# First attention: split values as the stationary operand, scaled probabilities of two token tiles as the moving one

## The reference, cut to what matters

```python
p = jax.nn.softmax(logits, axis=-1)
return jnp.einsum('bqhk,bqkhd->bqhd', p.astype(v.dtype), v_sel)
...
mixed = jnp.concatenate([a_out.reshape(b, s, D_A) * jax.nn.silu(za),
                         b_out.reshape(b, s, D_B) * jax.nn.silu(zb)], axis=-1)
x = x + jnp.einsum('bse,ed->bsd', mixed, w_out[layer])
```

## Time and profile before

| | |
|---|---|
| times of three runs | 1032.04, 1032.56, 1034.12 us; median 1032.56 us |
| the profiled execution | 1032.51 us, of which the span (first to last instruction) 1030.7 us |
| TensorE busy | 1019.2 us, 99% of the span |
| VectorE, ScalarE, GpSimd busy | 665.9 us (65%), 534.4 us (52%), 365.7 us (35%) |
| first attention (first score at 169.9 us, last value product ends just before 299.8 us) | TensorE busy 131.5 of the 132.5 us from 169.7 to 302.2 |
| second attention | 512 to 607 us, TensorE busy 93.5 of 95 us |

### The profile page before, as it was taken

The page is one execution under the profiler, slowest core; times in us unless marked ns, Lnnn a source line. Parts: engine busy times, 40 slices in busy tenths (PEclk is TensorE's granted clock), DMA queues, the critical chain, the costliest instruction groups (busy, mean ns, idle before and its releaser), DMA issues. The chain is left out here.

```text
span 1030.7 us, 14348 instructions
## 1 busy us (share of the span) xinstructions
PE 1019.2 (99%) x5310; PEld 843.8 (82%) x5310; DVE 665.9 (65%) x1141; ACT 534.4 (52%) x960; POOL 365.7 (35%) x334
## 2 busy tenths in 40 slices
PE   9999999999999999999999999999999999999997
PEld 7788888888878898988887788889888888888885
DVE  5578998675765346824567779444323325999996
ACT  7454445554673255545567884134434436554554
POOL 0022011003330001910165430007779965874562
PEclk9999999999999999999999999999999999999999
DMA  9655332314420285233200362239999951443552
GB/s 335 119 113 119 88 96 67 82 47 130 144 93 1 78 257 164 62 82 82 54 9 1 109 239 62 82 102 322 347 351 333 352 193 62 152 138 138 204 184 82
DMA packets 99637, 146.24 MB, mean 142 GB/s; under 512 B 6208, under 2 KB 60224, under 8 KB 99568
## 3 DMA queue, kind: packets, MB, share of 16 engines
q1 hardware_dynamic: 86016, 129.70, 38.6%
q10 hardware_dynamic: 12768, 12.88, 3.9%
q0 software_dynamic: 784, 2.75, 1.8%
HBM read 123.69 MB, written 21.63 MB: 141 GB/s over the span
## 5 line engine op out<-in xcount | busy, mean ns | idle before, releaser
L2462 DVE TENSOR_TENSOR w_lo<-wring,w_hi 128x1024 fp32r<-128x1024 f32 x32 | 53.0, 1658 | 105.8 <-ACT w_hi L1846 105.8
L1992 DVE TENSOR_TENSOR u_lo<-wring,u_hi 128x1024 fp32r<-128x1024 f32 (+1 forms) x64 | 80.8, 1272 | 50.9 <-ACT u_hi L1540 50.4
L869 PE MATMUL bank<-u_hi,h_hi 128*128 128x512 f32 (+1 forms) x288 | 111.0, 385 | 0.1
L869 PE MATMUL bank<-u_hi,h_lo 128*128 128x512 f32 (+1 forms) x288 | 109.4, 380 | 0.0
L869 PE MATMUL bank<-u_lo,h_hi 128*128 128x512 f32 (+1 forms) x288 | 109.1, 379 | 0.0
L1540 ACT ACTIVATE u_hi<-wring 128x1024 fp32r<-128x1024 f32 (+1 forms) x64 | 65.8, 1033 | 79.1 <-PE bank L869 57.2
L869 PE MATMUL bank<-h_hi,w_hi 128*128 128x512 f32 (+2 forms) x272 | 103.3, 380 | 0.0
L869 PE MATMUL bank<-h_hi,w_lo 128*128 128x512 f32 (+2 forms) x272 | 103.3, 380 | 0.0
L869 PE MATMUL bank<-h_lo,w_hi 128*128 128x512 f32 (+2 forms) x272 | 103.2, 380 | 0.0
L869 PE MATMUL bank<-h_hi,u_hi 128*128 128x512 f32 x224 | 94.4, 421 | 0.4 <-ACT arena L1482 0.2
L1370 PE MATMUL bank<-s_hi,f_hi 128*128 128x512 f32 x224 | 87.5, 391 | 0.7 <-DVE f_lo L2496 0.7
(11 more groups left out here) (374 smaller groups left out, 2543.7 us busy)
## 6 DMA issues: line engine op xcount, KB each, us to landing
wring<-in_w_in SPq DMA_DIRECT2D x60, 512.0 KB, 3.9
wring<-in_w_ff ACTq DMA_DIRECT2D x12, 1024.0 KB, 8.2
wring<-sums_kept SPq DMA_DIRECT2D x16, 768.0 KB, 4.2
wring<-in_w_ff SPq DMA_DIRECT2D x22, 512.0 KB, 6.2
wring<-in_w_ff SPq DMA_DIRECT2D x32, 256.0 KB, 3.3
sums_kept<-wring SPq DMA_DIRECT2D x22, 256.0 KB, 4.9
arena<-in_w_out SPq DMA_DIRECT2D x4, 1024.0 KB, 5.1
wring<-in_w_out SPq DMA_DIRECT2D x2, 2048.0 KB, 13.5
```

Of the source, the lines that this page charges most:

```text
L869: last = mm(b, lhs, rhs, start=(start and n == 0), stop=(stop and n == 2))
L1992: v.tensor_tensor(u_lo[u % RAW_UNITS][:, 0:cols], raw_unit(u), u_hi[u % HI_UNITS][:, 0:cols].bitcast(F32), ALU.subtract).then_inc(u_lo_don ...
L2462: v.tensor_tensor(cut(w_lo[ring3(m)]), src, cut(w_hi[ring3(m)]).bitcast(F32), ALU.subtract).then_inc(w_lo_done, 1)
```

## The change

What it does, part by part:

1. **Value products.** The values are kept split, high and low side by side (`v1_both`), and 128 columns of one head (64 high, 64 low) are the stationary operand. The transposed probabilities are split too (`pt1`), and are the moving operand: 256 columns for the key blocks that both token tiles of a pair (0, 1 or 2, 3) see, 128 for the last. `value1(o, n, r)` makes the whole output of one head for two token tiles. There are 192 matmuls in fp32r instead of 160 in f32.
2. **The output comes turned**, features on partitions. `mixed_transposes` goes. The products with the low halves come out in the upper 64 partitions: ScalarE copies those (`low_rows_of`), VectorE adds them to the lower ones (`collect1`, two additions a call).
3. **Scaling moves ahead of the transposes.** Since the division can't be made on turned outputs, VectorE takes the reciprocals of two steps (32 times) and GpSimd multiplies the 64 probability tiles by them (`scaled`). The transposes wait for `scaled`, and come two steps later than before, in loop t for steps t-4, t-3. The logits have eight buffers instead of four.
4. **Every transposed tile is written twice**, high by ScalarE (`turned_high`, 64 times) and low by VectorE (`turned_low`, 64 times), where one copy was made before.
5. **Room.** The split probabilities take places of the weight ring, so that the gate projections have two raw and two high places (`raw_place`, `hi_place`); their next unit is loaded when the last one but one is used up. Bias strips are loaded per round into two places. The values of vb and va are written by two activations a tile, their low halves by GpSimd (`value_low`). Part of the output weights moves (`late_raw`) and is loaded later, as are x and the first units of the second block.
6. **The end of the loop.** `WO_HIGH` and `ROW_AT` change, ScalarE makes the high half of piece 7 after its loop, the last `mix` is split in two halves, and `first_row` has another order.

```diff
-    WO_HIGH = {46: 0, 48: 1, 50: 2, 53: 3, 55: 4, 59: 5, 61: 6, 63: 7}
+    WO_HIGH = {48: 0, 49: 1, 50: 2, 53: 3, 55: 4, 60: 5, 61: 6}
-    ROW_AT = {58: ((0, 0),), 60: ((0, 1),), 62: ((0, 2),), 64: ((0, 4), (0, 5)), 66: ((0, 3), (1, 0))}
+    ROW_AT = {58: ((0, 0),), 60: ((0, 1),), 62: ((0, 2),), 64: ((0, 3), (0, 4)), 66: ((0, 5), (1, 0)), 68: ((1, 1), (1, 2))}
...
             def turn1(u):
-                pe.wait_ge(e_done, u + 1)
+                i = steps1[u][0]
+                pe.wait_ge(scaled, u + 1)
...
-                for j in range(i + 1):
-                    last = mm(bank[6 + o % 2][:, at:at + HD], probsT1[u % 2][:, j * P:(j + 1) * P],
-                              v1["v" + br][:, j, h * HD:(h + 1) * HD], start=(j == 0), stop=(j == i))
+                both = [(j, part) for j in range(end) for part in ("hi", "lo")]
+                order = both[:-1] + [(end, "hi"), (end, "lo")] + both[-1:]
+                for j, part in order:
+                    first, cols = (0, P) if j == end else (P * (2 * (end - j) - 1), 2 * P)
+                    at = 2 * P * (r + 1) - cols
+                    last = mm(bank[6 + q % 2][:, at:at + cols], v1_both[g][j // 2][:, j % 2, h, :, :].rearrange("p m d -> p (m d)"),
+                              pt1[n, part, r][:, first:first + cols], start=((j, part) == order[0]), stop=((j, part) == order[-1]))
                 last.then_inc(pv_done, 1)
-
-            def mixed_transposes(o):
...
+            for t in range(0, NS + 4, 2):
+                if t >= 4:
+                    turned_high(t - 4)
+                    turned_high(t - 3)
+                if t < NS:
+                    exps(t, steps1, 0, den, logits1)
+                    exps(t + 1, steps1, 0, den, logits1)
+                if t >= 10 and t % NH == 2:
+                    low_rows_of(2 * ((t - 10) // NH))
+                if t >= 16 and t % NH == 0:
+                    low_rows_of(2 * ((t - 16) // NH) + 1)
...
             for t in range(0, NS + 4, 2):
...
+                if t < NS:
+                    score1(t)
+                if 2 <= t < NS + 2:
+                    dve.wait_ge(e_done, t)
+                    v.reciprocal(den[:, t - 2:t], den[:, t - 2:t]).then_inc(rden_done, 1)
+                if t < NS:
+                    score1(t + 1)
+                if t >= 4:
+                    turned_low(t - 4)
+                    turned_low(t - 3)
+                if t >= 12 and t % NH == 4:
+                    collect1(2 * ((t - 12) // NH))
                 if t >= 18 and t % NH == 2:
+                    collect1(2 * ((t - 18) // NH) + 1)
                     mix((t - 18) // NH)
...
+            for u in range(NS):
+                if u % 2 == 0:
+                    pool.wait_ge(rden_done, u // 2 + 1)
+                g.tensor_scalar(logits1[u % 8], logits1[u % 8], den[:, u:u + 1], None, ALU.mult).then_inc(scaled, 1)
+                if u in (9, 11, 13, 15):
+                    value_low("va", (u - 9) // 2)
+                if u + 4 in combos:
+                    combine(u + 4)
```

More of the change, by code:

```diff
@@ L831, in unit_arrived @@
         def unit_arrived(eng, u):
-            eng.wait_ge(unit_in[u % RAW_UNITS], 16 * sum(len(units[m][3]) for m in range(u % RAW_UNITS, u + 1, RAW_UNITS)))
+            eng.wait_ge(unit_in[raw_place(u)], 16 * sum(len(units[m][3]) for m in range(u + 1) if raw_place(m) == raw_place(u)))
         def pair_arrived(eng, m):
@@ L2118, in finish1 @@
[L2118 to L2127 removed]
+                g = t // NH
@@ new lines, in collect1, with mix @@
+            def collect1(q):
+                o, n = q // 2, q % 2
+                dve.wait_ge(lo_rows_done, q + 1)
+                for r in range(2):
+                    cut = slice(2 * P * r, 2 * P * (r + 1))
+                    last = v.tensor_tensor(qk1[r * HD:(r + 1) * HD, o // 4, o % 4, OUTS, 2 * P * n:2 * P * (n + 1)],
+                                           bank[6 + q % 2][0:HD, cut], low_rows1[:, cut], ALU.add)
+                last.then_inc(o_free, 1)
+            def mix(o, cols=slice(0, S)):
@@ L2178, in _ @@
-                for f, tile, k in fill1:
-                    if f in (t, t + 1) and k == KC - 1:
+                for tile in FILL1:
+                    if GATE_AT[tile] in (t, t + 1):
                         gate_rows(tile)
@@ L2193, in _ @@
             mixed_low(6)
-            mix(7)
+            collect1(GROUPS - 2)
+            mix(7, slice(0, S // 2))
             dve.wait_ge(wo_lo_done, 9)
+            mixed_low(7, slice(0, S // 2))
             wo_low(9)
-            mixed_low(7)
-            for m in range(10, 14):
+            for m in (10, 11):
                 wo_low(m)
+            collect1(GROUPS - 1)
+            mix(7, slice(S // 2, S))
+            for m in (12, 13):
+                wo_low(m)
+            mixed_low(7, slice(S // 2, S))
             for u in range(2):
```

398 lines of the change are left out of this document (230 added, 168 removed).

## The result

The changed kernel takes 1068.85 us in the median of four runs (1068.37 to 1070.5), the kernel before in the same session 1032.98 us (1032.04 to 1034.12): a ratio of 1.035 (95%: 1.0332 to 1.0367). The direction is the one I gave the most chance, the size is not: 1038.0 was forecast, and even the upper end of the range, 1047, is 22 us too low.

A forecast was written before the change was run, and what follows sets the result against it. TensorE, busy 1019.2 of 1030.7 us, was taken as the bound. From 1032.5 us: less 17.8 of work and 2.0 of old waits, plus 8 of middle and 17.4 of end waits, gives 1038.1 us; range 1023 to 1047.

The forecast's parts named there:

- TensorE's work, -17.8 us: First attention: 160 f32 products and the mixed transposes removed, 192 products added; 17.8 us less work (16.0 to 17.9).
- the estimate beside it: Price of the 64 short value products by the Trainium skill's 81 ns per matmul: 5.2 us instead of 7.2.
- the page's two signs: Expected on the profile page: TensorE's busy time near 1000 us and its share of the span below 98%.
- Middle rounds of branch b: First attention before loop 56: waits of 0.7 us a round for scores queued behind VectorE's work.
- Middle rounds of branch a: First attention before loop 56: waits of 1.2 us a round, and 2 us in loop 52 behind two output-weight low halves.
- my high end of 13: Waits in the middle rounds, forecast at 8 us: 13 us if the weight ring's transfers come late.
- the two-place weight ring: Middle rounds: ScalarE waits for the next unit's transfer ahead of silu pairs, mostly covered by VectorE's waits; 1 us.
- no bound by itself: GpSimd in the first attention: 16 scalings of each size, 0.77 us for the largest, some 40 us in all.
- The end: Waits from loop 56 on, where no fill work is left: 17.4 us, of which 10.6 us need no backlog.
- P: Start of loop 56, 279.95 us in the trace before; TensorE was forecast to reach loop 64 at P + 14.1.
- Outside the stage: Edits outside the first attention cost nothing; 1 to 3 us if the cover for block two's first units is gone.
- Rival 4: Slower with lower clock: TensorE at 1.2 GHz after two waits of about 5 us, losing 2.5 us each; 1043 us, chance 0.15.

The follow-up runs named there:

- e10: e7 with the four silu pairs of this stage written as copies, leaving the activation out: 1040.26 us against 1042.76.
- e2: Changed kernel with the strips of group 6 and the next weight unit issued ahead of the first two output-weight loads on SP's queue: 1061.67 us.
- e1: Changed kernel with GpSimd's scaling of the probabilities given a second scalar, 1.0: 1062.04 us, 6.8 us less.
- e3: Changed kernel with both the two-scalar scaling and the weight unit issued ahead of the output weights: 1055.68 us.
- e5: e3 with the row terms of loops 64, 66 and 68 behind the transposes and value products instead of ahead: 1047.83 us.
- e9: Kernel before the change, with TensorE made to wait at loop 64 for a chain of three tiny transfers: 1040.03 us against 1032.91.
- e7: e5 with high halves of output weights at loops 47, 49, 51, 53, 55 and pieces 7 and 8 at loop 62: 1042.76 us, 1.0097 of the kernel before.
- e11: e7 with VectorE's `mix` moved from loops 2 modulo 8 to loops 4 modulo 8, behind the scores, except the last but one: 1044.25 us.
- e4: Changed kernel with 106 useless transposes filling TensorE's three long waits at the end of the first attention: 1063.25 us, 5.6 us less.
- e6b: e3 with high halves of output-weight pieces 0 to 4 at loops 50 to 58 and pieces 7 and 8 at loop 62: 1051.18 us.

## Why the prediction was right and wrong, step by step

- **TensorE's work, -17.8 us: borne out where it can be read.** Value products start 0.117 us apart, the short ones of 128 columns too, so the 64 of them are 7.5 us, for the 7.2 forecast and the 5.2 of the estimate beside it; a round of branch b without a long wait takes 15.0 us (212.94 to 227.93), and of that 0.77 us is a wait, which leaves 14.2 us, for the 14.1 forecast. Of the page's two signs, a share below 98% came true (96%) and TensorE near 1000 us busy failed: 1023.5, since work at the low clock is busy for about twice as long.

```profile
212.94 0.75 PEld L1081 LDWEIGHTS bank<-qk_half 64*128 64x128 f32 x12
...
224.04 0.54 PEld L1081 LDWEIGHTS bank<-qk_half 64*128 64x128 f32 x6 [0.77 <-DVE stats L2266]
...
227.93 0.19 PEld L1081 LDWEIGHTS bank<-qk_half 64*128 64x128 f32 x2
```

- **Middle rounds of branch b: right in size, in part by luck.** They take 15.3, 15.6 and 15.0 us, with 0.8 to 1.3 us of waiting in each, against "0.7 us a round" and rounds of "14.8 to 15.5 us". Only the waits at loops 22 and 30 (0.45 and 0.77 us) stand behind `collect1` and `mix`, as forecast; the one at loop 12 (1.18 us) stands behind the low half of a weight unit, and the one at loop 20 (0.84 us) behind a silu pair (see e10).
- **Middle rounds of branch a: mis-sized.** 1.2 us each and 2 in loop 52 were forecast; the rounds from 227.93 on take 18.7, 26.0 and 20.8 us. The waiting ahead of loop 56 is 20.6 us in all, outside even my high end of 13. Two links were seen and costed at almost nothing. "With the two-place weight ring ScalarE also waits for the next unit's transfer ... 1 us": it waits 7.64 us and TensorE 4.98, because I had not followed SP's queue past the two loads of output weights that the change puts ahead of it; e2 shows it. And GpSimd "no bound by itself" at 40 us: with 70.8 us of scaling it is busy for 14.8 of the 16 us from 232 to 248 us, and transposes wait for it 4.6 us in all; e1 shows it. The earlier trace rows are an instruction with two scalars, the new one has one; I took the shape for the form. (The totals of the other two were near: ScalarE 103.1 and VectorE 102.7 us up to the last value product, for 101 and 105; GpSimd has 104.1, where my terms add up to some 70.) The two low halves of output weights cost 2.94 us, for 2.
- **The end: right from loop 64 on, right by luck ahead of it.** The wait for piece 5 is 6.86 us (5.3 forecast; 4.85 in e3, where GpSimd has the speed that I had assumed), for piece 7 it is 5.24 and 0.76 us (4.8 and 0.6), for piece 9 2.50 us (2.2). Loop 64 comes up at P + 15.4 us, for P + 14.1, but not by the waits that I had named. Behind the silu, the transposes of step 56 wait only 0.20 us (2.1 forecast), and the scores of loop 62 wait 0.22 us (2.0 forecast). What came in their place are 0.91 and 1.82 us one loop earlier, where the transposes of steps 54 and 55 wait for GpSimd's scaling, and some 3 us of the low clock. (The terms of the forecast for the end add up to 17.3 us, not 17.4.) The forecast also took this end for a property of the change; e5 shows that 5 us of waits and about as much again through the clock were the order of TensorE's program.
- **Outside the stage: right.** 723.8 us against 723.6.
- **The clock: the step that failed most.** The sum has no term for it. Rival 4 had the mechanism, for two waits of 5 us, at a chance of 0.15, and for one such wait the right price, as e9 shows: 2.5 us, measured 2.7. It struck seven times, for 18.3 us: three times at waits that I had not foreseen (at 237, 261 and 299 us), four times at the very waits that I had forecast (2, 5.3, 4.8 and 2.2 us). Its rule, low for as long as the wait lasted, fits e9 but not this kernel: the clock stays at 0.50 for 6.9 us both at the wait of 2.94 us and at that of 6.86 us. By that rule the four forecast waits at loop 52, piece 5, piece 7 and piece 9 would have cost 1.0 + 2.7 + 2.4 + 1.1 us and made the forecast 1045 us, still inside my range: to miss by 22 us at its upper end it took both failures, the clock's and the middle's. Once a forecast has waits of that length, the clock belongs into its sum and not into a rival. The Trainium skill (TensorE: Matmul & The Clock Gate, section "HAM oscillation — how this bites in real kernels") describes matmul bursts that start at half speed after waits of 3 to 5 us for transfers; the trace of the changed kernel agrees for all its waits of 2.5 us and more. At shorter ones it shows both: the clock fell at 237.9 us, behind 1.27 and 0.74 us, and not behind 1.18 us at 189.39 us.

Of the 30 us between forecast (5.5 us slower) and result (36 us slower), 18.3 us are the clock (forecast: nothing), 12.6 us the waits of the middle (20.6 for 8), 1.6 us those of the end (19.0 for 17.4); the sum is 2 us too high, as above. All of the change's disadvantage is waits and clock; with the four edits of e7, 26 of the 36 us are gone, and what is left are short waits before score pairs and transposes that only change places (e11).

## What to carry to other kernels

Where TensorE has no slack, as here, moving its work to engines that run in order turned busy time into waits, and the waits were charged about one and a half times (7.1 us for one of 5.0 in e9; 39.6 us of waits and 18.3 us of lost clock in the changed kernel), since the work behind them starts at 1.2 GHz: price that as part of the sum. Follow every queue past which a transfer is moved, with its bytes, not only the engines' totals. And take an instruction's price from a row with the same operands, not only the same shape.

## What the hardware did that I had not expected

- GpSimd's multiplication by a column of scalars takes 1.56 us for 128x512 with one scalar and 0.72 us with a second scalar of 1.0 behind it; for 384, 256 and 128 columns 1.27, 1.01 and 0.60 against 0.59, 0.51 and 0.37 us. Why is open.
- After a wait of 5.0 us the clock stays at 0.50 over 5.3 us of gapless work (e9). It also fell at 237.9 us of the changed kernel, behind waits of only 1.27 and 0.74 us close together; but in e4, with 1.46 and 0.74 us at the same place, it stayed at 1.00, and so it did behind a wait of 2.96 us in e6b, up to the next wait (282 to 290 us):

```profile
232.00:250.00 18.00, 14.06 (x92) 10.83 (x90) 12.20 (x36) 10.13 (x28) 16.54 (x16) 1.00 0.31 94
```

- Most kernels with such waits differ more between runs: 1052.91 to 1062.58 us in e3, with mean clocks from 0.991 down to 0.981, and 1038.58 to 1043.98 in e10, against at most 3.4 us among the runs of the kernel before in any one session. It is no rule: e7, which has such waits too, stays within 0.6 us, with mean clocks from 0.994 to 0.997.
